# Two-layer blocks on one core: the split of turned heads into high and low parts stands last in each place of three attentions, and one gate spread stands in another place

## The reference, cut to what matters

```python
def joint_dense_attention(q, k, v, kc, vc):          # gqa and mla: all 512 + 256 keys
    ...
    sc = jnp.einsum('bqkgd,bnkd->bkgqn', qi, kk, ...) * (d ** -0.5)
    p = jax.nn.softmax(sc, axis=-1)
    return jnp.einsum('bkgqn,bnkd->bqkgd', p.astype(vv.dtype), vv)

def ab_layer(...):
    ...
    mix = jnp.concatenate([oa, ob], axis=-1) * jax.nn.silu(g)
    x = x + gate * (mix @ w_out)

def cd_layer(...):                                    # win: a band of 3 blocks of 128 keys and the context
    ...
    mix = jnp.concatenate([oc, od], axis=-1) * jax.nn.silu(g)
    x = x + gate * (mix @ w_out)
```

## Time and profile before

| what | before |
|---|---|
| median of 3 runs | 1555.17 us (1554.95 to 1555.58) |
| the profiled execution, its own time | 1554.78 us |
| its span, first to last instruction | 1553.0 us |
| TensorE busy | 1487.5 us (96%) |
| VectorE busy | 850.9 us (55%) |
| ScalarE busy | 677.9 us (44%) |
| GpSimd busy | 592.3 us (38%) |
| chain that ended last | PE 81%, DVE 7%, POOL 5%, ACT 3%, issue 3% |
| mean granted clock of TensorE | 0.998 |

### The profile page before, as it was taken

The page is one execution under the profiler, slowest core; times in us unless marked ns, Lnnn a source line. Parts: engine busy times, 40 slices in busy tenths (PEclk is TensorE's granted clock), DMA queues, the critical chain, the costliest instruction groups (busy, mean ns, idle before and its releaser), DMA issues.

```text
span 1553.0 us, 25078 instructions
## 1 busy us (share of the span) xinstructions
PE 1487.5 (96%) x9488; PEld 1240.5 (80%) x9488; DVE 850.9 (55%) x1879; ACT 677.9 (44%) x1377; POOL 592.3 (38%) x349
## 2 busy tenths in 40 slices
PE   4999998898999999999899999999999999999998
PEld 3778787787888878888788889967788788877887
DVE  4573708876764265933742997056322599617322
ACT  3333336565566353335744333467323433346332
POOL 1212223691005553447725444423234444430244
PEclk9999999999999999999999999999999999999999
DMA  9657620000012333331013323300233233310322
GB/s 326 181 140 192 175 62 27 2 2 1 2 35 89 108 109 96 95 95 42 28 33 94 96 82 98 93 14 28 69 93 106 75 99 101 96 41 1 109 82 95
DMA packets 103717, 128.61 MB, mean 83 GB/s; under 512 B 10608, under 2 KB 63792, under 8 KB 103600
## 3 DMA queue, kind: packets, MB, share of 16 engines
q1 hardware_dynamic: 103600, 127.01, 27.4%
HBM read 124.90 MB, written 2.10 MB: 82 GB/s over the span
## 4 chain that ended last, share of the span: by engine, by line
PE 81%; DVE 7%; POOL 5%; ACT 3%; issue 3%; DMA 1%; SPq 1%; DVEq 0%; ACTq 0%; POOLq 0%
PE psum L1048 21%; PE psum L1050 20%; PE psum L1049 20%; PE psum L1293 3%; PE psum L1236 3%; PE psum L1004 2%; PE psum L1215 2%; PE psum L1151 1%; PE psum L1340 1%; PE psum L1322 1%; PE psum L1272 1%; POOL rx L2403 1%; POOL mla_q L2403 1%; DVE psum L1943 1%; PE psum L1273 1%
## 5 line engine op out<-in xcount | busy, mean ns | idle before, releaser
L2353 POOL TENSOR_TENSOR wlo<-wraw,whi 128x1024 fp32r<-128x1024 f32 (+4 forms) x181 | 413.1, 2283 | 704.6 <-ACT whi L1445 704.6
L1445 ACT ACTIVATE whi<-wraw 128x1024 fp32r<-128x1024 f32 (+4 forms) x181 | 181.6, 1003 | 421.7 <-PE psum L1050 415.4
L1048 PE MATMUL psum<-whi,h2h 128*128 128x512 f32 (+2 forms) x800 | 309.5, 387 | 2.6 <-DVE h2l L1959 1.5
L1050 PE MATMUL psum<-whi,h2l 128*128 128x512 f32 (+2 forms) x800 | 305.2, 382 | 0.0
L1049 PE MATMUL psum<-wlo,h2h 128*128 128x512 f32 (+2 forms) x800 | 304.6, 381 | 0.0
L1048 PEld LDWEIGHTS psum<-whi,h2h 128*128 128x128 f32 x800 | 150.3, 188 | 28.5 <-issue 2.7
L1050 PEld LDWEIGHTS psum<-whi,h2l 128*128 128x128 f32 x800 | 150.2, 188 | 27.1
L1049 PEld LDWEIGHTS psum<-wlo,h2h 128*128 128x128 f32 x800 | 150.4, 188 | 24.8
L1048 PE MATMUL psum<-whi,hTh 128*128 128x512 f32 (+2 forms) x372 | 143.4, 385 | 3.7 <-DVE hTl L1959 2.7
L1050 PE MATMUL psum<-whi,hTl 128*128 128x512 f32 (+2 forms) x372 | 136.2, 366 | 0.0
L1049 PE MATMUL psum<-wlo,hTh 128*128 128x512 f32 (+2 forms) x372 | 135.8, 365 | 0.0
(11 more groups left out here) (391 smaller groups left out, 2956.4 us busy)
## 6 DMA issues: line engine op xcount, KB each, us to landing
rx<-mod_w_in SPq DMA_DIRECT2D x32, 512.0 KB, 5.1
wraw<-w_in_odd_in SPq DMA_DIRECT2D x32, 512.0 KB, 3.6
wraw<-cd_w_in_in SPq DMA_DIRECT2D x24, 512.0 KB, 3.7
wraw<-w_in_even_in SPq DMA_DIRECT2D x20, 512.0 KB, 3.7
wraw<-ab_w_out_in SPq DMA_DIRECT2D x16, 512.0 KB, 3.7
wraw<-w_ple_gate_in SPq DMA_DIRECT2D x16, 512.0 KB, 3.8
mod_w_even<-mod_w_in SPq DMA_DIRECT2D x8, 512.0 KB, 10.3
wraw<-ab_w_in_in SPq DMA_DIRECT2D x8, 512.0 KB, 8.3
```

The lines of the kernel that those rows point to most:

```text
L1048: eng.matmul(dst, a[0], ww[0], start=first, stop=False)
L1050: mm = eng.matmul(dst, a[1], ww[0], start=False, stop=last_)
L1445: eng.activation(hi_of(u)[:, :, 0:w], wraw[:, u["id"] % RAW, :, 0:w], ACT.Copy).then_inc(*to("split_hi", u["id"]))
L2353: eng.tensor_tensor(lo_of(u)[:, :, 0:w], wraw[:, u["id"] % RAW, :, 0:w], f32(hi_of(u)[:, :, 0:w]), ALU.subtract)\
```

## The change

Three moves; no instruction is added, removed or resized.

- ScalarE: the high parts of the heads turned in place j come after the copy of probabilities and the exponentials of that place, not before them.
- VectorE: the low parts of these heads come after the copy of probabilities, the mix and the inverse of that place, not right after the maximum. The work `beside(j)` still stands last.
- The second half of the second layer's gate is spread after `win` place 6 (copied by ScalarE at the head of place 7), not after place 9.

TensorE's own order is the same but for the spread.

```diff
@@ -353,7 +353,7 @@
         spread_at = {("gqa", 5): (0, 0, 0), ("gqa", 7): (0, 0, 1), ("gqa", 9): (0, 1, 0), ("gqa", 21): (0, 1, 1),
-                     ("win", 3): (1, 0, 0), ("win", 9): (1, 0, 1)}
+                     ("win", 3): (1, 0, 0), ("win", 6): (1, 0, 1)}
@@ -1620,14 +1620,14 @@
                 for j in range(len(units) + 4):
                     if (name, j - 1) in spread_at:
                         spread(*spread_at[name, j - 1])
-                    for what in preps_at(name, j):
-                        prep(*what)
                     if 2 <= j < len(units) + 2:
                         copy_probs(name, j - 2, turned_probs(name, j - 2), (name, (j - 5) // 2) if j >= 5 else None)
                     if j < len(units):
                         if j >= 3:
                             probs_free(name, j - 3)
                         exponentials(name, j, probs(name, j))
+                    for what in preps_at(name, j):
+                        prep(*what)
                     if (name, j) in LEADS:
                         lead, n_ = LEADS[name, j]
                         split_hi(ahead_of(lead)[n_])
@@ -2110,8 +2110,6 @@
                 for j in range(len(units) + 4):
                     if j < len(units):
                         maximum(name, j)
-                    for what in preps_at(name, j):
-                        low(*what)
                     if 2 <= j < len(units) + 2:
                         copy_probs(name, j - 2, turned_probs(name, j - 2), (name, (j - 5) // 2) if j >= 5 else None)
                     m, r = divmod(j - 5, 2)
@@ -2126,6 +2124,8 @@
                         eng.wait_ge(*at("exps", (name, 2 * m + 1)))
                         c_, r_ = 2 * m % 4, 2 * (m % 4)
                         eng.reciprocal(rinv[:, r_:r_ + 2], rsum[:, c_:c_ + 2]).then_inc(*note("vector", ("inverse", name, m)))
+                    for what in preps_at(name, j):
+                        low(*what)
                     beside(j)
```

## The result

The changed kernel takes 1581.03 us (median of four, 1580.08 to 1581.90), the kernel before 1555.38 on the same chip: 1.0166 times as long, 95% interval 1.0150 to 1.0181. That is 25.7 us slower. 18.6 were forecast, and 1581.03 lies outside the range of 1566 to 1580. The profiled execution took 1581.88 us, with a span of 1580.1, 27.1 more than before. Of all executions behind the numbers of this document, one, of the kernel with VectorE's move in `win` alone, was slow at 5656 us, and its ratio leaves it out.

A forecast was written before the change was run, and what follows sets the result against it. VectorE's root for the norms was taken to bound the kernel until 354.60, then TensorE itself. Terms 12.6 + 6.1 + 1.6 - 1.7 gave 18.6 us slower, 1573.8 us, with a range of 1566 to 1580.

The forecast's parts named there:

- the loop through bank 7: Turned head, high part, low part, next turn gets longer: 12.6 us lost in `mla`, 6.1 in `gqa` places 40 to 47.
- the term for `win`: In `win`: 1.1 us won by the spread, 0.7 each at places 13 and 17, 0.8 lost at place 1; together 1.7 won.
- gqa places 40 to 47: End of `gqa`, a head turned in every place: five stalls of 1.0 to 1.5 us, sum 6.1 us, bounds 4.5 to 7.
- gqa places 0 to 9: Start of `gqa`, VectorE the bound: later low parts in places 2 and 4 delay the root 1.6 us, bounds 0.6 and 2.5.
- The step for GpSimd: Start of `gqa`: the later root makes GpSimd's row of norms 1.6 us later, its first scaling starting near 291.2.
- What TensorE gains or loses before 354.60 counts for nothing: In `gqa` before `mla`'s first head turns: VectorE's root sets the end until 354.60, so TensorE's own changes are priced at nothing.
- The other heads of `gqa` stand two places apart and cost nothing: Remaining `gqa` heads: the four to five microseconds of two places cover the longer loop, so no loss.
- the 1.4: `win` places 13 and 17: the two halves no longer delay the copy TensorE waits for, 0.7 us won at each.
- a fall: TensorE's clock falls for the 24 us from 354 to 378, at most 24 us more, 1598 us; 2% chance.
- mild: Half of the stalls are caught up because later units find maximum and exponentials done: +9 us, 1564; 8% chance.
- the faster one: Earlier exponentials let TensorE keep a third of its `gqa` and `mla` idle time: some 7 us faster, 1547; 5% chance.
- The cascade: From `gqa` place 40 on, later low parts delay VectorE's next maximum, 0.5 us for each of 32 heads: 1590 us; 5% chance.

The follow-up runs named there:

- the three filled runs in `mla`: Identity turns added in stalls: six each, kernel before with `mla` first-of-pair parts late, 1568.28 us; eight or five each, whole change, 1579.66 and 1579.65 us.
- the last and the first heads of pairs in `mla`: Kernel before with `mla` high and low parts late only where no head is turned in the next place, 1555.98 us; only where one is, 1570.24 us.

## Why the prediction was wrong

The direction was right, and so was the loop through bank 7, which made two of the four terms; the size was 7 us short. In medians the parts cost 15.3, 6.7, 2.0 and 0.9 us where 12.6, 6.1, 1.6 and -1.7 were priced. So 2.6 of the missing 7.1 us belong to the term for `win` and 2.7 to `mla`, where the stalls were priced well and the sum had left the clock at 2.4 GHz; 0.8 is in no part. By the prediction's own steps:

- **The loop through bank 7 in mla,** 12.6 priced: 12.2 at full clock. That the cover of a pair's second head is enough is shown (1555.98), and so is that nearly all the loss is at the first heads.
- **gqa places 40 to 47,** 6.1 priced: 6.1 at full clock (30.3 less 24.2). The stalls stand in places 42, 43, 44, 46 and 47, as named. The whole change has one more, 0.53 us in place 41 (at 361.24), which was held to be covered.
- **gqa places 0 to 9,** 1.6 priced: 2.7 in the profile, 2.0 in medians. The step for GpSimd was right (1.5 to 1.75 later). Two others failed. One is "What TensorE gains or loses before 354.60 counts for nothing": TensorE had 1.41 us of slack there, by its own wait on GpSimd, and came 4.0 us later (353.19, that is 354.60 less 1.41, against 357.16). The other is "The other heads of `gqa` stand two places apart and cost nothing": 2.5 of the 4.0 us come from them, in places 20 to 30. That the total is near the price is luck; it was made elsewhere.
- **win,** -1.7 priced: +2.4 in the profile, +0.9 alone. This is the step with the wrong sign. The spread's 1.1 us gave 0.1 by itself. Places 9 and 11, priced at nothing, cost some 0.8 (836.8 less the 1.6 of the stretch, against the 834.4 with the spread alone); place 1 cost 0.9 where I had 0.8. At places 13 and 17 the 1.4 was argued from one wait for ScalarE's copy: it went, waits for VectorE's copies and for exponentials took its place, and some 0.6 was won. The run with VectorE's move alone has that wait unchanged and gains 2.0 us. The gain was there to be had, but from VectorE's order, and ScalarE's late high parts took it back.
- **The clock.** The sum left TensorE at 2.4 GHz, and a fall had 2%, at the end of `gqa` only and for 24 us. What came is of another shape: single stretches of 3.4 us, in `mla` (2.5 us in the changed profile), `gqa` (7.3 less 6.1, and less the wait in place 41, so 0.7 at 364.4) and `win` (1.6).

Put together for the profiled execution: 27.1 less 18.6 is 8.5 us, of which the clock after place 40 has 4.8 (0.7, 2.5, 1.6), `win`'s stalls 2.6 (0.9, not -1.7), the start of `gqa` 1.1, the wait in place 41 0.5, and `mla`'s stalls -0.4; that makes 8.6. The medians differ by less, 25.7: the profiled execution was the second longest of the four.

The rivals: no gain was kept in `gqa` or `mla`, and nothing was caught up (mild). For the faster one, a third of 17.3 us is 5.8 and not 5.5, and 7 us less is 1548; neither matters to the forecast. The cascade didn't happen from `gqa` place 40 on, where the stalls explain the time, though place 28 has a piece of it. ScalarE's move alone shows it, 29 us above the whole change; the later low part, which I took for its cause, is what prevents it.

For the clock, the Trainium skill's "TensorE: Matmul & The Clock Gate", section "A second HAM failure mode: psum-queue depth-cycling", has the rule that spoke against me: a kernel that cycles through PSUM banks idles between groups of matmuls and can see the gate go back and forth between its two rates. The prediction looked at the section on oscillation beside it and set it aside because no row of `gqa` showed it. The rows at 0.50 above agree with the rule, and so do the three filled runs in `mla`, where the gaps were filled and no such stretch came.

## What to carry to other kernels

Before moving a step back in an engine's order, look for the loop that it closes: who must have its result before a shared buffer is written again, and how soon that writer comes; the same move was nearly free in `mla` where the writers came two places apart, and cost some 1.2 us where they came in adjacent places (12.2 us at ten stalls). Even with two places between, look at what else stands behind the moved step on its engine: in `gqa` the maximum and the copy of the next place came late. Price moves on two engines apart as well as together: here ScalarE's alone cost 54 us, VectorE's 4, both 26, and VectorE's in one stage alone gained 2. Where stalls of a microsecond come into a stage that had none, add a term for TensorE's clock, and count slack in microseconds before calling a loss hidden.

## What the runs showed of the hardware

The granted clock of TensorE fell to 0.50 (1.2 GHz) for 3.4 us at a time after idle gaps of 1.3 to 2.0 us: at 364.40 after waits of 0.53 and 1.99 us at 361.24 and 364.10, at 395.20 after one of 1.79 at 393.34, at 483.90 after one of 1.63 at 483.44, at 750.10 after one of 1.28 at 750.01. Each stretch in `mla`, at the end of `gqa` and in `win` cost 0.7 to 1.6 us; those at the start of `gqa`, in the changed kernel and in the run of that part, cost nothing that can be seen at place 12. Which of the equal stalls was followed by one differed between executions: four in one profile of `mla`, one in another. Nor does a stretch need the change: with `gqa` as before, four profiles have one from 270.5, 270.9 or 271.2 on (the spread alone, the last and the first heads of pairs in `mla`, `win` places 13 and 17), behind two waits of TensorE like those that the kernel before has there (1.24 and 0.62 us, at 269.06 and 270.30). What decides which gap is followed by one stays open.

The kernel holds a guard of its own: in `win` places 0 and 1 TensorE turns the identity 4 and 10 times (`KEEP`, L463), before the change and after it. The filler of the experiments is the same idea, put where the stalls were new.

The executions of the kernel before lie in two groups, about 1555.0 and 1556.1. In the profiles the difference is there before `gqa` begins: the same sum of squares of VectorE (L2252), in the first places, starts at 264.0 to 264.4 in some and at 265.0 to 265.7 in others, whatever stands behind it. So effects of 1 us were read from stretches of a profile and not from its end; what makes the two groups isn't known.
